# Hybrid pooling and sparse-attention layer on one core: query norms in single steps, three raw weight buffers, masks three units earlier, output gate built in pieces

## What is computed

```python
mod = silu(c) @ w_ada + b_ada                       # shift, scale, gate: 3 x 1024
h = rmsnorm(x, norm_gain) * (1 + scale) + shift
proj = h @ w_in                                     # 4808 columns
(u_a, z_a, q, k, v, z_b, q_idx, k_idx, w_idx, g_a, g_b) = split(proj)
y_a = multiscale_pool(u_a, w_pool_group, pool_scale) * silu(z_a)
q = rope(rmsnorm(q per head, q_norm_gain)); k = rope(rmsnorm(k, k_norm_gain))
score = sum_h relu(q_idx[h] @ k_idx.T) * w_idx[h]   # causal
keep the 256 best keys of each query; 8-head attention with one shared key and value head
y_b = attn * silu(z_b)
merged = sigmoid(g_a) * (y_a @ w_branch_a) + sigmoid(g_b) * (y_b @ w_branch_b)
x + gate * (merged @ w_out)
```

## Time and profile before

| what | value |
| --- | --- |
| median of 3 runs | 886.59 us |
| profiled execution, its own time | 887.66 us |
| span of its instructions | 885.9 us |
| TensorE busy | 823.7 us (93%) |
| VectorE busy | 602.1 us (68%) |
| ScalarE busy | 338.3 us (38%) |
| GpSimd busy | 330.1 us (37%) |
| mean granted TensorE clock | 0.978 |

### The profile page before, as it was taken

How to read it: one execution, slowest core, us unless ns; L and a number is a source line. 1 busy time by engine, 2 the same in 40 slices (tenths; PEclk the granted TensorE clock), 3 DMA queues, 4 the chain that set the end, 5 groups by cost and what they waited for, 6 DMA issues and landing times.

```text
span 885.9 us, 14117 instructions
## 1 busy us (share of the span) xinstructions
PE 823.7 (93%) x5038; PEld 723.5 (82%) x5042; DVE 602.1 (68%) x1275; ACT 338.3 (38%) x613; POOL 330.1 (37%) x288
## 2 busy tenths in 40 slices
PE   3899989895999999999999999799999999989998
PEld 3699988885998888887788877688888887869998
DVE  5835448896888888888884251377778894765542
ACT  6463434663222222223231221576667761320100
POOL 1024634345212577862652212653322002772010
PEclk9799999997999999999999999799999999999999
DMA  9830111002331321331123214432311005945432
GB/s 359 308 96 2 48 48 37 13 24 60 107 95 48 95 95 48 95 95 47 48 84 96 95 60 143 142 120 87 105 49 60 13 3 170 328 148 193 136 96 72
DMA packets 62560, 87.96 MB, mean 99 GB/s; under 512 B 5754, under 2 KB 44190, under 8 KB 61600
## 3 DMA queue, kind: packets, MB, share of 16 engines
q10 hardware_dynamic: 28100, 41.96, 14.1%
q1 hardware_dynamic: 32476, 38.86, 14.0%
q0 software_dynamic: 1920, 6.29, 1.9%
HBM read 66.12 MB, written 20.97 MB: 98 GB/s over the span
## 4 chain that ended last, share of the span: by engine, by line
PE 70%; issue 8%; DVE 7%; POOL 4%; DMA 4%; ACT 3%; DVEq 2%; SPq 1%; POOLq 1%; ACTq 1%
PE pp L550 19%; PE pp L551 19%; PE pp L552 19%; PE pp L860 3%; PE pt L843 3%; DMA ada_w<-in_w_ada 2%; DVEq L1892 1%; PE ps L688 1%; PE ps L687 1%; PE pt L871 1%; DVE pT L1839 1%; DVE logit L1922 1%; DVE m_raw L1907 1%; POOLq L1386 1%; POOL w_lo L490 1%
## 5 line engine op out<-in xcount | busy, mean ns | idle before, releaser
L490 POOL TENSOR_TENSOR w_lo<-w_raw,w_hi 128x1024 fp32r<-128x1024 f32 x50 | 121.4, 2445 | 241.5 <-ACT w_hi L485 190.9
L1776 DVE TENSOR_SCALAR_CACHE_REDUCE junk<-score,cand 128x384 uint8<-128x384 f32 (+1 forms) x186 | 168.6, 944 | 19.3 <-issue 13.3
L550 PE MATMUL pp<-hT_hi,w_hi 128*128 128x512 f32 x384 | 150.4, 392 | 0.0
L552 PE MATMUL pp<-hT_hi,w_lo 128*128 128x512 f32 x384 | 149.5, 389 | 0.0
L551 PE MATMUL pp<-hT_lo,w_hi 128*128 128x512 f32 x384 | 149.5, 389 | 0.0
L550 PE MATMUL pp<-w_hi,hT_hi 128*128 128x256 f32 x352 | 102.7, 292 | 9.7 <-POOL w_lo L490 8.2
L551 PE MATMUL pp<-w_lo,hT_hi 128*128 128x256 f32 x352 | 100.8, 286 | 0.0
L552 PE MATMUL pp<-w_hi,hT_lo 128*128 128x256 f32 x352 | 100.6, 286 | 0.0
L550 PEld LDWEIGHTS pp<-hT_hi,w_hi 128*128 128x128 f32 x384 | 72.1, 188 | 16.1 <-issue 0.8
L552 PEld LDWEIGHTS pp<-hT_hi,w_lo 128*128 128x128 f32 x384 | 72.1, 188 | 15.2
L551 PEld LDWEIGHTS pp<-hT_lo,w_hi 128*128 128x128 f32 x384 | 72.1, 188 | 14.5
(11 more groups left out here) (268 smaller groups left out, 1829.6 us busy)
## 6 DMA issues: line engine op xcount, KB each, us to landing
w_raw<-in_w_in SPq DMA_DIRECT2D x36, 512.0 KB, 3.7
ada_w<-in_w_ada SPq DMA_DIRECT2D x7, 1024.0 KB, 11.6
sgb_spill<-stage ACTq DMA_DIRECT2D x16, 256.0 KB, 2.0
sga_spill<-stage ACTq DMA_DIRECT2D x16, 256.0 KB, 2.0
stage<-sga_spill ACTq DMA_DIRECT2D x16, 256.0 KB, 2.9
ma_spill<-stage POOLq DMA_DIRECT2D x16, 256.0 KB, 2.4
e_in<-sgb_spill ACTq DMA_DIRECT2D x16, 256.0 KB, 4.9
e_in<-ma_spill ACTq DMA_DIRECT2D x16, 256.0 KB, 6.3
```

What stands on the lines that cost most here:

```text
L490: nc.gpsimd.tensor_tensor(lo, raw, hi.bitcast(F32), ALU.subtract).then_inc(w_lo_done, 1)
L550: nc.tensor.matmul(o, a_hi, b_hi, start=first, stop=False)
L552: return nc.tensor.matmul(o, a_lo, b_hi, start=False, stop=last)
L1776: v.tensor_scalar(junk[:, n % 2, 0:keys(b)], score[:, score_at(b):score_at(b + 1)], least, None, ALU.is_ge, ALU.add, accum_out=cnt[:, n:n ...
```

## The change

- `RAW` is 3: piece n is loaded once piece n-3 has its `w_lo`. Piece 4 is loaded ahead of `wg_raw`, and ScalarE rounds piece 5 directly behind piece 4, ahead of `qi_tile(0, 2)`.
- Query norms: blocks 2 to 5 carry one tile each (tiles 0 to 3), one step after each of heads 2, 3, 5, 6 and 7. Tiles 4 to 7 come after the loop: all squares and means, then root, scale and gain tile by tile. ScalarE's roots of tiles 4 to 7 stand ahead of the `zb` tiles. GpSimd's last four `finish_query` come behind the `w_lo` splits of `zb` 0 and 1, which therefore wait for no query tile in blocks 6 and 7.
- `MASK_UNIT` is 5 to 10.
- The reloads of `stage` buffers 0, 1 and 2 are issued after `ga` units 13, 14 and 15; only the fourth is left ahead of attention.
- The gate vector is made in eight pieces of two rows during attention: load 0 ahead of `q_split_hi(0)`, `gate_add(n)` on VectorE behind `logit` in step 4n+4, load n+1 on ScalarE in step 4n+6, the two `gate_rows` products in steps 18 and 34. Nothing of it is left in the merge and output phases.
- Buffers are laid out anew for this (`gate_w` has two rows, `gate_acc` both halves), and the scratch for GpSimd's DMAs is 4096 instead of 8192.

```diff
-    RAW = 2
+    RAW = 3
-    MASK_UNIT = {8 + n: FREE_BLOCKS + n for n in range(NSEL)}
+    MASK_UNIT = {5 + n: FREE_BLOCKS + n for n in range(NSEL)}
+    GATE_STEP = {4 * n + 4: n for n in range(8)}
+    GATE_ROWS = {18: 0, 34: 1}
...
-        NORM_AT = {(FREE_BLOCKS, 1): 0, (FREE_BLOCKS, 4): 1}
-        NORM_AT.update({(b, 2): b - 1 for b in range(FREE_BLOCKS + 1, NT)})
+        NORM_IN = range(FREE_BLOCKS, FREE_BLOCKS + 4)
+        NORM_TILE = {b: b - FREE_BLOCKS for b in NORM_IN}
+        NORM_LATE = range(len(NORM_IN), NT)
...
+            query_steps = {2: query_squares, 3: query_means, 5: query_rsqrt, 6: query_scale, 7: query_gain}
...
-                    if (b, h) in NORM_AT:
-                        norm_query(NORM_AT[b, h])
-                    if (b, h) in SCALE_AT:
-                        scale_query(SCALE_AT[b, h])
+                    if b in NORM_IN and h in query_steps:
+                        query_steps[h](NORM_TILE[b])
...
+            for t in NORM_LATE:
+                query_squares(t)
+                query_means(t)
+            for t in NORM_LATE:
+                query_rsqrt(t)
+                query_scale(t)
+                query_gain(t)
...
                 for u in range(4):
                     gate_unit("ga", i, u)
+                    if i == 3 and u:
+                        load_sga(u - 1)
...
-            for n in range(4):
-                load_sga(n)
+            load_sga(3)
+            act.wait_ge(bias_ready, NSEL + 1)
+            act.dma_start(gate[0:1, :], b_ada[:, 2 * D:3 * D]).then_inc(gate_row_in, 16)
+            load_gate(0)
...
+                if i - 2 in GATE_STEP and GATE_STEP[i - 2] + 1 < 8:
+                    load_gate(GATE_STEP[i - 2] + 1)
+                if i in GATE_ROWS:
+                    gate_copy(GATE_ROWS[i])
...
+            def gate_add(n):
+                g, j = n // 4, n % 4
+                acc = gate_acc[:, g * HALF:(g + 1) * HALF]
+                dve.wait_ge(gate_in, 16 * (n + 1))
+                for u in range(2):
+                    c = c_silu[:, 2 * j + u:2 * j + u + 1]
+                    if j == 0 and u == 0:
+                        ins = v.tensor_scalar(acc, gate_w[:, u, :], c, None, ALU.mult)
+                    else:
+                        ins = v.scalar_tensor_tensor(acc, gate_w[:, u, :], c, acc, ALU.mult, ALU.add)
+                    if u == 0:
+                        dve.drain()
+                ins.then_inc(gate_used, 1)
+                if j == 3:
+                    dve.wait_ge(gate_row_in, 16)
+                    dve.drain()
+                    own = gate_acc[0:1, g * HALF:(g + 1) * HALF]
+                    v.tensor_tensor(own, own, gate[0:1, g * HALF:(g + 1) * HALF], ALU.add).then_inc(gate_sum, 1)
...
+                if i in GATE_STEP:
+                    gate_add(GATE_STEP[i])
```

More of the change, by code:

```diff
@@ L201, in hybrid_layer @@
             pt_uses.append((("out", (i - 4) // 4), "v"))
+        if i in GATE_ROWS:
+            pt_uses.append((("gate", GATE_ROWS[i]), "a"))
         if YB_STEP.get(i) == NT - 1:
             pt_uses.append((("yb", NT - 1), "av"))
-    pt_uses += [(("gate", g), "a") for g in range(2)]
     pt_at, pt_done, na, nv = {}, [], 0, 0
@@ L468, in _ @@
             load_x(7)
+            load_piece(4)
             sp.dma_start(wg_raw[:], w_group.rearrange("g c d -> c g d")).then_inc(group_in, 16)
-            for n in range(4, len(pieces)):
+            for n in range(5, len(pieces)):
                 load_piece(n)
@@ L873, in _ @@
                     last.then_inc(pt_full, 1)
+                if i in GATE_ROWS:
+                    g = GATE_ROWS[i]
+                    pe.wait_ge(gate_sum, g + 1)
+                    nc.tensor.matmul(pt_claim(("gate", g))[:], ones[:], gate_acc[:, g * HALF:(g + 1) * HALF],
+                                     start=True, stop=True).then_inc(pt_full, 1)
                 for _ in range(WB_AFTER.get(i, 0)):
@@ L999, in _ @@
             scale(5)
-            split_piece_hi(act, 5)
             qi_tile(0, 3)
@@ L1179, in load_sga @@
                 act.dma_start(stage[:, n % 4, :], sga_dram[r:r + P, f * HALF:(f + 1) * HALF]).then_inc(sga_in[n % 4], 16)
+            for i in range(4):
+                for u in range(4):
+                    gate_unit("ga", i, u)
+                    if i == 3 and u:
+                        load_sga(u - 1)
+                    if 4 * i + u in MASK_UNIT:
+                        tie_copy(MASK_UNIT[4 * i + u])
+                split_chunk_hi(act, name_of[("ga", i)] + 2)
             def branch_a_copy(n):
@@ L1228, in q_copies, with load_gate, gate_copy @@
                                          ACT.Copy).then_inc(pt_free_a, 1)
-            def load_gate(g, j):
-                if g and j == 0:
-                    act.wait_ge(gate_sum, g)
-                act.dma_start(gate_w[:, 2 * j:2 * j + 2], w_ada.rearrange("(p k) n -> p k n", k=KD)[
+            def load_gate(n):
+                g, j = n // 4, n % 4
+                if n:
+                    act.wait_ge(gate_used, n)
+                act.dma_start(gate_w[:], w_ada.rearrange("(p k) n -> p k n", k=KD)[
                     :, 2 * j:2 * j + 2, 2 * D + g * HALF:2 * D + (g + 1) * HALF]).then_inc(gate_in, 16)
-                if j == 3:
-                    act.dma_start(gate[0:1, g * HALF:(g + 1) * HALF],
-                                  b_ada[:, 2 * D + g * HALF:2 * D + (g + 1) * HALF]).then_inc(gate_in, 16)
+            def gate_copy(g):
+                o = pt_take(("gate", g))
+                nc.scalar.activation(gate[:, g * HALF:(g + 1) * HALF], o[:], ACT.Copy).then_inc(pt_free_a, 1)
             act.wait_ge(pp_full, PP_HT)
```

99 lines of the change are left out of this document (30 added, 69 removed).

## The result

The changed kernel takes 897.66 us (median of 4 runs, 896.89 to 899.45), the kernel before 885.86 us beside it: ratio 1.0139, 95% interval 1.0116 to 1.0162. That is 11.8 us slower; 7.5 us faster was forecast (879.1 against 886.59). The profiled execution of after took 899.45 us, its span is 897.7 us.

A forecast was written before the change was run, and what follows sets the result against it. TensorE, busy 823.7 of 885.9 us, was taken as the bound. Front -5.0, reloads -5.5, gate +9.5 and end -6.5 summed to -7.5 us: profiled 880.2, median 879.1, own range 875 to 884, whole range 871.5 to 887.5.

The forecast's parts named there:

- Start: Ahead of the first index tiles: piece 5 rounded first removes GpSimd's and TensorE's stands, minus 1.6 us.
- Index loop: Index blocks 2 to 7: with norms moved, TensorE leaves some 12 us earlier, VectorE's last score comes about 11 us earlier.
- what comes late: VectorE between last score and bisection: four norms where it had one, 23.3 us where before it was 15.3.
- From the bisection's start to its ties: Masks: TensorE 11 us earlier, ties only 4.7, so a new wait of 4.4 us at unit 5, plus 1.6 for half clock.
- Rival (d): Behind the index loop: every w_lo and rotation holds VectorE, front gives only 1 us; put at 885 us, chance 0.11.
- Reloads: Ahead of attention: earlier stage reloads bring query copies and first S forward; minus 5.5 us, bounds 3 and 7.
- Gate in pieces: During attention: gate additions exposed at steps 8, 16, 24 and 32, GpSimd holds, products; plus 9.5 us, bounds 2 and 13.
- End: Merges and output: VectorE no longer shared with the gate, products gone; minus 6.5 us, bounds 4 and 7.
- (a): Masks: no new wait at unit 5; up to 6 us more gained, 873.1 us, chance 0.13.
- (b): Attention: gate pieces fit into the gaps and cost only their 2.1 us of products; 871.7 us, chance 0.13.
- (c): Attention: gate pieces land late and VectorE waits in gate_add, 12 us showing; 891.1 us, chance 0.11.
- front: From the start through the masks: minus 5.0 us in all, bounds minus 1 and minus 11.

The follow-up runs named there:

- m8: The changed kernel with the mask products back at unit 8 and on, nothing else: 881.70 us, 0.9954 of the kernel before.
- m8_start: m8 with raw buffers, load order and rounding at the start as before the change: 885.76 us.
- m8_norm: m8 with the query norms placed as before the change, on all engines: 892.81 us.
- gom8_rel: gate_old_m8 with all four reloads of stage issued behind the query loads, as before the change: 873.37 us.
- gate_old: The changed kernel with the gate vector built as before the change: 883.39 us.
- m8_g8: m8 with the eight gate pieces at steps 4, 12, 20, ... 60, products at steps 30 and 62: 869.65 us.
- gate_old_m8: The changed kernel with the gate vector built as before the change and masks at unit 8 and on: 872.06 us, 0.9817 of the kernel before.
- b_m5: The kernel before the change with only the masks moved to unit 5 and on: 884.81 us, 0.9996 of the kernel before.
- m8_gend: m8 with seven gate pieces at steps 4, 12, ... 52, the eighth at step 65, products at steps 65 and 67: 868.33 us.
- m8_d10: m8 with ten repeated squares on VectorE ahead of the late roots, so that the bisection begins later: 884.92 us.

## Why the prediction was wrong, step by step

*Start: right in kind, its size not shown.* 1.6 us forecast, 2.1 us in the traces of m8 and m8_start, which is within the scatter of the first loads. In the traces of before and after, both at the first score at 122.2, it didn't show.

*Index loop: right.* Waits for `rel` fell from 9.8 to 0.4 us, the first `zb` tile had no gap, and the third waited 9.55 us for ScalarE behind the last root, as written (some 10 us). The last score ended 10.1 us earlier (11 forecast, and 1.6 from the start). m8_norm puts the norms' whole worth at 11.1 us, 9.3 by the ratios.

```profile
210.74 0.58 PE L551 MATMUL pp<-w_hi,hT_hi 128*128 128x256 f32 x1 [9.55 <-ACT zb_out L1038]
```

The bisection began 3.9 us earlier, between the 3.1 and the 4.7 of the text. Two misses offset each other there: VectorE left the loop 10.1 us earlier and not 12.6, and what comes late took 21.5 us and not 23.3.

*From the bisection's start to its ties: the first step that failed.* "After the change TensorE is there 11 us earlier, the ties only 4.7" took the bisection for 249.6 us of work that moves as a block. It doesn't: GpSimd's splits set when its late rounds go on, and in whole rounds. The ties came 4.5 us later, an error of 9.2 us. TensorE's lead at unit 5 was 9.3 and not 11, so the wait was 11.9 and not 4.4 us, and the low clock behind it cost 4 x 0.50 + 4 x 0.20 = 2.8 and not 1.6 us. In all 14.7 us, and 16.0 by m8, where the forecast had 6.0 (4.4 + 1.6). Rival (d) had the right place, VectorE held by GpSimd, and the wrong time of it: it charged the holds behind the loop, not in the 31 rounds.

*Reloads: mis-sized.* 5.5 us forecast (3 to 7), measured 1.3 us in the medians and 2.7 by the first `logit` (gom8_rel), or 4 by the ratios. GpSimd's wait of 2.73 us did go, but the first S waits for the query copies. I had added the gain of one queue to that of another that runs beside it; that this is the reason is argued, not shown. With the gate pieces in, the first `logit` comes 1.6 us (after against gate_old) to 2.4 us (m8_g8 against gate_old_m8) later again.

*Gate in pieces: the second step that failed.* The mechanism was right, at the steps that were named: gaps ahead of L861 at steps 9, 17, 25 and 33, little at 12, 20 and 28. Its size was not. The forecast was 9.5 us, 2 to 13; it cost 18.4 us by position, beyond its upper bound, and 14.3 us net of the end by gate_old, where the text has 9.5 - 6.5 = 3.0. Steps 8, 16, 24 and 32, to which the text gives 6.2 us (1.3, 2.1, 1.2, 1.6, with no row behind them) and 1.3 for GpSimd, took 2.3, 4.8, 1.3 and 3.6 us more than before, 12.0 in all. Mis-sized terms: GpSimd's holds, 1.3 us in the text, are 15.7 - 14 x 0.75 = 5.2 us on the additions (two of the holds, 2.7 and 1.7 us, in steps that were exposed anyway). The products, 2.1 us in the text, made each of their two steps 1.4 to 2.9 us longer in after and m8, against 0.8 us in m8_g8; probably since they share the transposes' banks and VectorE is behind by then. And the clock was 0.62 over the 4 us behind the stand of 4.6 us, where the text charged a low clock only at the masks. Counting each step's spare time in the trace, as was done for m8_g8, would have put the pieces elsewhere.

*End: right in size.* 6.5 us forecast, 7.0 to 7.2 by position. From step 63 on it is 159.4 us in the kernel before, 157.4 in gate_old and gate_old_m8, 152.3 in after and 150.7 in m8. So 5.1 to 6.7 us are the gate's, and the other 2 scatter: b_m5, with the end of before, has 157.5 too.

*The rivals.* (a), no new wait, and (b), pieces that fit, didn't happen here; m8_gend is (b) at other steps. (c), late loads, was one wait of 0.77 us.

In sum, against the profiled execution: front 7.7 us worse than forecast, reloads and ramp 3.5, gate in attention 8.9, end 0.5 better. That is 19.6 us, and the profiled time is 899.45 - 880.2 = 19.3 us above its forecast.

## What to carry to other kernels

Before a wait is moved ahead, ask what its two sides will do once the rest of the change has worked: the mask place cost nothing in the kernel before (b_m5) and 16 us behind a lead of 9 us and ties 4.5 us late. Work for an engine that is not the bound goes where that engine's spare time lies, step by step (seven places in attention made the gate cost 1.7 us there instead of 18.3), and away from another engine's long instructions. The length of a loop of dependent small steps is not a constant when another engine can hold them: find the last instruction that holds it, and count whole rounds behind that.

## What the runs showed of the hardware

A VectorE step of 0.23 us on 128x6 elements lasts 2.17 or 2.18 us beside a GpSimd `w_lo` of 2.38 us in the rows above (up to 2.39 us in m8_start), and ends when that ends; two in a row are held by one `w_lo` each. The big counts of the rounds are not held (the 128x1024 one takes 1.27 us beside a `w_lo` and without). In m8_d10 this turned 8.2 us of extra work on VectorE into no delay. A one-partition addition of 0.68 us can be held to 3.26 us as well as a full one.

The Trainium skill, SBUF — State Buffer, section "Who interferes with whom", says that whichever of the two engines issues first gets the port pair that they share for its whole instruction, and that the other blocks fully. The small steps of these traces agree (2.17 against 2.38 us), and so do the means behind the index loop, held to 1.67 and 1.39 us in the changed kernel, not to the 4.22 us of the earlier trace rows that the prediction preferred. But a hold isn't always over with one instruction. The mean of the earlier trace rows stayed through the second of two `w_lo`, that of m8_norm, 9.13 us, through four, and the gate addition at 595.43 lasted 3.44 us, 2.7 more than alone, through the `w_lo` and into the `y_row` behind it. What decides between one instruction and several, no run here shows.
